# Moving the copies of two decode states from the ConvFFN stages into the prompt-attention stages

## The chip, the cores and the metric

The kernel runs on one core of one Trainium2 chip. The metric is device time in microseconds (us) for one execution, and a version is judged by its median over several runs.

## The reference

One inference step of a two-layer decoder trunk for a prompt (512 tokens) and a group of 8 samples with 8 new tokens each (T = 576 tokens in all). Layer 0 mixes with A (indexer-selected attention) and B (dilated windows), layer 1 with C (compressed, selected and sliding-window branches); each layer ends in a ConvFFN:

```
def conv_ffn(x, prev, w_up, conv_w, conv_b, w_down):
    n = x.shape[1]
    ext = jnp.concatenate([prev, x @ w_up], 1)
    ...
    return (jax.nn.gelu(gate) * val) @ w_down, ext[:, n:]
```

The step also returns its states, shifted by the 8 new rows. Only this part of the reference is what the change touches:

```
    kv_b = jnp.concatenate([state_kv, jnp.stack([kb, vb], 2)], 1)      # (8, 2048 + 8, 1024 floats)
    ... kv_b[:, -B_BUF:]                                               # s_b_kv, the last 2048 rows
    win = jnp.concatenate([state_win, kv[:, :, 4:]], 1)                # (8, 512 + 8, 256 floats)
    ... win[:, -C_BUF:]                                                # s_c_win, the last 512 rows
```

So 2040 rows of 4 KB for each of 8 samples of state_b (66.8 MB), and 504 rows of 1 KB for each sample of state_c (4.1 MB), are copied unchanged from one DRAM tensor to another. No engine computes with the copies.

## The kernel before

The kernel is a list of phases. Each opens its own SBUF and PSUM tiles and one block with a program for each engine (SyncE is SP, the others PE, DVE, ACT, POOL), and ends when every engine's program has ended: the semaphores are cleared, and all engines meet at a barrier (L97, L101). The order is: setup, projection of A and B, token-major rearrangement, indexers, sample attention B, sample attention A, prompt attention `pab`, output projection, `ffn0`, projection of C, rearrangement, compressed prompt branch, prompt attention `pc`, sample attention C, output projection, `ffn1`.

`ffn_phase` has an up part and a down part. The up part is a loop of LOOPS = 11 steps. A step has two slots s, and a slot holds 8 x 128 rows by 256 columns of w_up (1 MB, two loads of 512 KB by SP at L1633, tile `ffn_w`). ACT casts the slot to its high part (L1753, `ffn_wh`), DVE subtracts to get the low part (L208, `ffn_wl`), and PE forms three products for each (L216): 48 matmuls of 288 columns for each half slot, 192 in a step. SP may load a slot again as soon as DVE has split what was in it (`sp.wait_ge(w_low, ...)`). ACT may cast it as soon as PE has finished the slot's former content. ACT and DVE then do the convolution and the gate. The down part takes 22 pieces of w_down (512 KB each, SP at L1642, four slots), split in the same way (L1795, L208), and 30 matmuls of 512 columns for each (L1725 to L1727).

The copies are in the up part. At the start of each of the 11 steps ACT issues one DMA for four samples at once (L1558):

```
        e.dma_start(self.dst_b[self.b, bass.ds(i * self.ROWS, self.ROWS), :],
                    self.src_b[self.b, bass.ds(i * self.ROWS + NS, self.ROWS), :]).then_inc(self.copied, 16)
```

The access pattern is 4 samples x 185 rows x 4 KB. After the steps come a rest of 5 rows and the copy of state_c (L1564, L1565), and at the end of the phase ACT waits for them all. `ffn0` copies samples 0 to 3, `ffn1` samples 4 to 7.

`prompt_attention_phase` runs over 16 heads. In `pab` these are 8 heads of B and then 8 heads of A, with 4 query tiles each (per_head = 4). In `pc` each head has two branches (per_head = 8). PE computes logits (L560), DVE adds the bias from a table and takes the maximum (L639), ACT exponentiates (L620), PE turns (L571) and multiplies by the values (L588). SP loads a table of 1280 KB for each four heads and branch (L539), and for each head its queries, 128 KB in a ring of three slots (L543):

```
                if n >= 3:
                    sp.wait_ge(logit_ready, per_head * (n - 2))
                sp.dma_start(q[:, n % 3, :], hT[q_row:q_row + HD, 0:SEQ]).then_inc(q_in[n % 3], 16)
```

So the queries of head n are asked for when the logits of head n - 3 are done, two heads before PE needs them. After the last of them SP has nothing to do in the phase.

Of the kernel before, what the change touches and what calls it, by code (L numbers as in the profile page):

```python
# [26 lines left out]
NB, NS = 8, 8  # L27
# [5 lines left out]
PAST = 2048  # L33
PAGE = 128
LS = PAST + NS
HD = 64
# [36 lines left out]
class Phase:  # L73


    def __init__(self, nc, ctx, name):
        self.nc, self.ctx, self.name, self.sems = nc, ctx, name, []
        self.body = ExitStack()
# [405 lines left out]
                dve.tensor_tensor(s, s, keep.causal[:, :], ALU.add).then_inc(summed, 1)  # L484


def prompt_attention_phase(nc, name, branches, heads, hT, vec_up, tok, keep, tok_loads=(), sel_bias=None):

# [4 lines left out]
    with phase(nc, name) as p:  # L495
# [17 lines left out]
                 "weighed", "scaled", "mixed", "k_scaled")  # L513
        logit_ready, shifted_ready, probs_ready, turned, pT0, pT1, out_ready, weighed, scaled, mixed, k_scaled = (p.sem(n) for n in names)
        pT_ready = [pT0, pT1]
        k_in, v_in = p.sem("k_in"), p.sem("v_in")
        q_in = [p.sem(f"q_in{i}") for i in range(3)]
        t_in = [p.sem(f"table_in{i}") for i in range(2 * parts)]
        steps = [(n, i, part) for n in range(len(heads)) for i in range(NQ) for part in range(parts)]
# [3 lines left out]
        @block.sync  # L523
        def _(sp):
            for br, b in enumerate(branches):
                rows = hT[b["k"]:b["k"] + b["kv"] * HD, 0:SEQ].rearrange("(g e) t -> e g t", e=HD)
                sp.dma_start(kT[:, br, 0:b["kv"], :], rows).then_inc(k_in, 16)
            for n, (q_row, place, members) in enumerate(heads):
                if n == 1:
                    for dst, src in tok_loads:  # L530
                        sp.dma_start(dst, src).then_inc(v_in, 16)
                if n % 4 == 0:
                    g = n // 4
                    if g >= 2:
                        sp.wait_ge(shifted_ready, 4 * per_head * (g - 1))
                    for part, (br, h) in enumerate(members):
                        slot = (g % 2) * parts + part
                        head0 = (branches[br]["kind"] * N_HEADS + branches[br]["h0"] + h) * LU
                        sp.dma_start(table[:, slot, :, :], bass.AP(tensor=vec_up.tensor, offset=head0,  # L539
                                                                   ap=[[1, P], [LU, 4], [1, SEQ + P]])).then_inc(t_in[slot], 16)  # L540
                if n >= 3:
                    sp.wait_ge(logit_ready, per_head * (n - 2))
                sp.dma_start(q[:, n % 3, :], hT[q_row:q_row + HD, 0:SEQ]).then_inc(q_in[n % 3], 16)  # L543

        @block.tensor
        def _(pe):
# [999 lines left out]
class StateCopy:  # L1546

    ROWS = (PAST - NS) // (NF // 2)  # L1550

    def __init__(self, io, half, copied):
        self.src_b, self.dst_b, self.src_c, self.dst_c = io["state_b_kv"], io["o_s_b_kv"], io["state_c_kv"], io["o_s_c_win"]
        self.b, self.copied, self.before = slice(half * NB // 2, (half + 1) * NB // 2), copied, half * 16 * (NF // 2 + 2)

    def step(self, e, i):

        e.dma_start(self.dst_b[self.b, bass.ds(i * self.ROWS, self.ROWS), :],  # L1558
                    self.src_b[self.b, bass.ds(i * self.ROWS + NS, self.ROWS), :]).then_inc(self.copied, 16)

    def rest(self, e):

        done = self.ROWS * (NF // 2)
        e.dma_start(self.dst_b[self.b, done:PAST - NS, :], self.src_b[self.b, NS + done:PAST, :]).then_inc(self.copied, 16)  # L1564
        e.dma_start(self.dst_c[self.b, 0:C_WIN - NS, :], self.src_c[self.b, NS:C_WIN, :]).then_inc(self.copied, 16)  # L1565

    def wait(self, e):

        e.wait_ge(self.copied, self.before + 16 * (NF // 2 + 2))


def ffn_phase(nc, name, w_up, conv_w, conv_b, w_down, prev, g, b, p_tail, s_tail, y, state_copy, keep):

# [10 lines left out]
    with phase(nc, name) as p:  # L1586
# [172 lines left out]
        @block.scalar  # L1759
        def _(act):  # L1760
            act.wait_ge(up_done, 4)
            for s in range(2):
                split_high(act, s, 0, s)

            def step(i, ahead):

                state_copy.step(act, i)
                for s in range(2):
                    for e in (2 * s, 2 * s + 1):
                        act.wait_ge(up_done, i * 4 + (e + 5))  # L1770
                        act.wait_ge(conv3, i * 4 + (e + 1))
                        act.wait_ge(tails_out, i * 8 + 2 * (e + 1))
                        act.copy(ext[:, e, 2:2 + TH], acc[e][:, 0:TH]).then_inc(main_out, 1)
                    if ahead:
                        split_high(act, i * 2 + (s + 2), i + 1, s)
                    for e in (2 * s, 2 * s + 1):
                        act.wait_ge(main_out, i * 4 + (e + 5))
                        act.wait_ge(small_out, i * 8 + 2 * (e + 5))
                        act.wait_ge(prefix_in, i * 8 + 2 * (e + 1))
                        act.wait_ge(hid_done, i * 4 + 2 * (s + 1))  # L1780
                        act.activation(conv[:, e, :], ext[:, e, 0:CV], ACT.Identity, scale=par_slot[:, e, 0:1], bias=par_slot[:, e, 3:4]).then_inc(conv1, 1)
                    act.wait_ge(conv3, i * 4 + (2 * s + 5))
                    act.activation(gelu[:, s, :], conv[:, 2 * s, :], ACT.Gelu_apprx_tanh).then_inc(gelu_done, 1)

            with act.Fori(0, LOOPS - 1) as i:
                step(i, True)
            step(LOOPS - 1, False)
            state_copy.rest(act)
            act.wait_ge(hid_done, 4 + 2 * NF)
            for n in range(NF):  # L1790
                f2 = n % (NF // 2)
                down_slot_free(act, n)
                act.copy(hh[:, n % 3, :, 0:T], hid[:, 2 * f2:2 * f2 + 2, :]).then_inc(d_high, 1)  # L1793
                act.wait_ge(wd_in[n % 4], 16 * (n // 4 + 1))
                act.copy(wdh[:, n % 4, :, :], wd[:, n % 4, :, :]).then_inc(d_high, 1)  # L1795
                if 3 <= n < NF // 2 + 3:
                    m = n - 3
                    act.wait_ge(tail_turned, m + 1)
                    if m >= 2:
                        act.wait_ge(tail_stored[m % 2], 32 * (m // 2))  # L1800
                    act.copy(tail_rows[:, m % 2, :], acc2[1 + m % 2][0:NR, :]).then_inc(tail_out, 1)
                    act.wait_ge(tail_out, m + 1)
                    act.dma_start(p_tail[:, m * 512:(m + 1) * 512], tail_rows[0:2, m % 2, :]).then_inc(tail_stored[m % 2], 16)
                    act.dma_start(s_tail[:, m * 512:(m + 1) * 512], tail_rows[2:NR, m % 2, :]).then_inc(tail_stored[m % 2], 16)
            for t in range(NT):
                norm.root_of(act, t)
            for t in range(NT):
                norm.scale(act, t)
                if t >= 2 and y is None:
                    norm.high_part(act, t - 2, acc2[1:3])  # L1810
            if y is None:
                for t in range(NT - 2, NT):
                    norm.high_part(act, t, acc2[1:3])
            state_copy.wait(act)
            for m in range(2):
                act.wait_ge(tail_stored[m], 32 * len(range(m, NF // 2, 2)))

# [726 lines left out]
def build(nc, io):  # L2544
# [7 lines left out]
    with ExitStack() as ctx:  # L2552
# [7 lines left out]
        keep.causal = sb("causal", [P, P])  # L2560
        keep.chunk_row = sb("chunk_row", [P, NB], I32)
        keep.eps = sb("eps", [P, 1])
        copied = ctx.enter_context(nc.semaphore("state_copied"))
        const_in = ctx.enter_context(nc.semaphore("const_in"))

        keep.kidx_in = [ctx.enter_context(nc.semaphore(f"kidx_in{b}")) for b in range(NB)]
# [23 lines left out]
        with ExitStack() as ab:  # L2590
# [12 lines left out]
            with ExitStack() as pr:  # L2603
# [4 lines left out]
                    dict(heads=H_B, k=B_K, kv=H_B, v=P, kind=KIND_DIL, h0=8, sel=False, gate=None),  # L2608
                    dict(heads=H_A, k=A_K, kv=2, v=0, kind=KIND_FULL, h0=0, sel=True, gate=None),
                ], [(B_Q + h * HD, H_A + h, [(0, h)]) for h in range(H_B)] + [(A_Q + h * HD, h, [(1, h)]) for h in range(H_A)],  # L2610
                    dram.hT_ab, dram.vec_up, v_tok, keep, tok_loads=[
                    (v_tok[:, :, 0:P], io["o_p_a_kv"].rearrange("(i p) c -> p i c", p=P)[:, :, P:2 * P]),
                    (v_tok[:, :, P:], io["o_p_b_kv"][3 * SEQ:, :].rearrange("(i p) c -> p i c", p=P)[:, :, 512:D]),
                ], sel_bias=sel_bias)
        with x_parts(nc, keep, "x1"):
            output_phase(nc, "out_ab", io["w_out_ab"], io["ln1_g"][0], io["ln1_b"][0], keep)
            ffn_phase(nc, "ffn0", io["ffn_up"][0], io["ffn_conv_w"][0], io["ffn_conv_b"][0], io["ffn_down"][0], io["state_ffn"][0],
                      io["ln2_g"][0], io["ln2_b"][0], io["o_p_ffn"][0], io["o_s_ffn"][0], None, StateCopy(io, 0, copied), keep)

            project_phase(nc, "proj_c", io["w_in_c"], C_COLS, dram.hT_c, keep)  # L2620

        with ExitStack() as c:
# [6 lines left out]
            with nc.sbuf_tensor("mix_c", [P, NQ, D], F32) as mix:  # L2629
# [2 lines left out]
            prompt_attention_phase(nc, "pc", [  # L2632
                dict(heads=N_HEADS, k=C_KV + 2 * P, kv=2, v=3 * P, kind=KIND_FULL, h0=0, sel=False, gate=N_HEADS),
                dict(heads=N_HEADS, k=C_KV + 4 * P, kv=2, v=5 * P, kind=KIND_WIN, h0=0, sel=False, gate=2 * N_HEADS),
            ], [(C_Q + h * HD, h, [(0, h), (1, h)]) for h in range(N_HEADS)], dram.hT_c, dram.vec_up, tok, keep)
        sample_c_phase(nc, dram.hT_c, dram.vec, io["cache_c_kv"], io["state_c_kv"], io["o_s_c_kv"],
                       io["o_s_c_win"][:, C_WIN - NS:C_WIN, :], io, keep)
        with x_parts(nc, keep, "x2"):
            output_phase(nc, "out_c", io["w_out_c"], io["ln1_g"][1], io["ln1_b"][1], keep)
            ffn_phase(nc, "ffn1", io["ffn_up"][1], io["ffn_conv_w"][1], io["ffn_conv_b"][1], io["ffn_down"][1], io["state_ffn"][1],  # L2640
                      io["ln2_g"][1], io["ln2_b"][1], io["o_p_ffn"][1], io["o_s_ffn"][1], (io["o_y_prompt"], io["o_y_sample"]),
                      StateCopy(io, 1, copied), keep)


def t5_buckets(dist):
# [85 lines left out]
```

## Time and profile before

| | |
|---|---|
| time, 3 runs | 3455.67 us median, 3441.11 to 3469.64 |
| span of the profiled execution | 3459.9 us |
| PE busy | 2655.9 us (77%) |
| DVE / ACT / POOL busy | 1477.0 / 885.0 / 177.5 us |
| bytes moved by DMA | 344.26 MB, mean 100 GB/s |
| mean granted TensorE clock | 0.824 |

The profile gives no time of its own for the profiled execution beside its span. All times below are microseconds from the start of that span. The prompt attention `pab` runs from about 846 to 1032, `ffn0` from 1122 on, `pc` from about 1993 to 2304, and `ffn1` from 2822 to the end. The page cuts the span into 40 slices of 86.5 us and gives, in tenths, the busy share of an engine, the granted TensorE clock and the mean busy share of the 16 DMA engines.

### The profile page before, as it was taken

To read this page: it belongs to the slowest core of one execution; us is meant where nothing else is said; L and a number is where in the kernel's file an instruction comes from. 1 tells how busy PE (TensorE), PEld (TensorE's weight loads), DVE (VectorE), ACT (ScalarE), POOL (GpSimd) and SP (SyncE) were. 2 spreads that over 40 slices of the span, in tenths; PEclk is the share of its full clock that TensorE was granted. 3 is DMA by queue.
4 is the path that set the end of the run, shared out by engine and by line. 5 is a ranking of instruction groups with operands and counts; after the bars stand their busy time and mean duration, and the time that the engine had idled before them with its cause. 6 is when DMAs were issued, how large, how long until landed. Compare 5 with 4: busy or idle time off the path is not lost. (4 is left out here: it accounts for less than half of the span.)

```text
span 3459.9 us, 38384 instructions
## 1 busy us (share of the span) xinstructions
PE 2655.9 (77%) x13798; PEld 2027.6 (59%) x13802; DVE 1477.0 (43%) x2970; ACT 885.0 (26%) x1465; POOL 177.5 (5%) x404
## 2 busy tenths in 40 slices
PE   5976788686987777667967889977777777667596
PEld 2973333253556777666867745544555567667585
DVE  2223577555455333342342234654344433343334
ACT  1111111111232332233221122432323222333232
POOL 0000000000000111110000000000000011111000
PEclk9997788787588888879978556988889778888898
DMA  3352544222111433342123121133212123334321
GB/s 88 129 192 71 203 149 153 88 98 75 42 35 55 147 132 130 132 152 93 44 94 98 32 75 37 41 79 119 98 67 110 61 60 130 137 131 144 132 82 46
DMA packets 208838, 344.26 MB, mean 100 GB/s; under 512 B 32982, under 2 KB 144646, under 8 KB 204786
## 3 DMA queue, kind: packets, MB, share of 16 engines
q1 hardware_dynamic: 194992, 204.40, 19.5%
q10 hardware_dynamic: 10268, 83.75, 5.9%
q0 software_dynamic: 3456, 54.53, 4.1%
q8 instruction: 71, 1.16, 0.1%
q14 instruction: 51, 0.42, 0.0%
HBM read 315.74 MB, written 97.35 MB: 119 GB/s over the span
## 5 line engine op out<-in xcount | busy, mean ns | idle before, releaser
L216 PE MATMUL ffn_acc<-x_h,ffn_wh 128*128 128x288 f32 x1408 | 313.6, 306 | 217.5 <-DVE ffn_wl L208 217.5
L216 PEld LDWEIGHTS ffn_acc<-x_h,ffn_wh 128*128 128x128 f32 x1408 | 236.7, 197 | 220.0 <-issue 220.0
L208 DVE TENSOR_TENSOR ffn_wl<-ffn_w,ffn_wh 128x2048 fp32r<-128x2048 f32 (+1 forms) x88 | 154.4, 1754 | 410.8 <-ACT ffn_wh L1753 345.8
L216 PE MATMUL ffn_acc<-x_l,ffn_wh 128*128 128x288 f32 x1408 | 310.2, 303 | 0.0
L216 PE MATMUL ffn_acc<-x_h,ffn_wl 128*128 128x288 f32 x1408 | 309.5, 303 | 0.0
L216 PEld LDWEIGHTS ffn_acc<-x_l,ffn_wh 128*128 128x128 f32 x1408 | 236.0, 196 | 0.0
L216 PEld LDWEIGHTS ffn_acc<-x_h,ffn_wl 128*128 128x128 f32 x1408 | 235.2, 196 | 0.0
L1725 PE MATMUL ffn_acc<-ffn_wh,x_h 128*128 128x512 f32 x440 | 177.3, 403 | 69.2 <-DVE ffn_wl L208 69.2
L1726 PE MATMUL ffn_acc<-ffn_wl,x_h 128*128 128x512 f32 x440 | 174.6, 397 | 0.0
L1727 PE MATMUL ffn_acc<-ffn_wh,x_l 128*128 128x512 f32 x440 | 174.2, 396 | 0.0
L1753 ACT CAST ffn_wh<-ffn_w 128x2048 fp32r<-128x2048 f32 x44 | 84.0, 1910 | 316.8 <-DMA ffn_w<-ffn_up 316.8
L560 PE MATMUL pc_logit<-pc_kT,pc_q 64*128 64x128 f32 (+3 forms) x256 | 127.9, 589 | 15.7 <-DMA pc_q<-hT_c 15.7
L1725 PEld LDWEIGHTS ffn_acc<-ffn_wh,x_h 128*128 128x128 f32 x440 | 84.7, 193 | 87.6 <-DVE ffn_wl L208 40.5
L208 DVE TENSOR_TENSOR x_l<-ffn_hid,x_h 128x1152 fp32r<-128x1152 f32 x44 | 59.7, 1357 | 154.5 <-ACT x_h L1793 154.5
L639 DVE CUSTOM_DVE_ANT_0 pc_shifted<-pc_logit,pc_table 128x128 f32<-128x128 f32 (+3 forms) x128 | 62.7, 490 | 145.2 <-PE pc_logit L560 144.9
L620 ACT ACTIVATE pc_probs<-pc_shifted,pc_nmax 128x128 f32<-128x128 f32 (+3 forms) x128 | 71.9, 562 | 194.6 <-DVE pc_nmax L639 194.6
L588 PE MATMUL pc_out<-pc_pT,tok_c 128*64 128x128 f32 x640 | 118.9, 328 | 0.0
L2195 PE MATMUL sc_tps<-ident,sc_kv 128*128 128x128 f32 x384 | 67.5, 329 | 50.7 <-DMA sc_kv<-cache_c_kv,chunk_row 25.2
L1201 PE MATMUL sb_outp<-sb_v,sb_pT 128*64 128x512 f32 x160 | 91.4, 740 | 8.8 <-DVE sb_pT L1298 8.8
L588 PEld LDWEIGHTS pc_out<-pc_pT,tok_c 128*64 128x64 f32 x640 | 82.1, 162 | 25.7 <-issue 22.8
L1793 ACT CAST x_h<-ffn_hid 128x1152 fp32r<-128x1152 f32 x44 | 50.8, 1155 | 174.7 <-PE ffn_acc L1727 171.2
L1727 PEld LDWEIGHTS ffn_acc<-ffn_wh,x_l 128*128 128x128 f32 x440 | 84.6, 192 | 18.1
(404 smaller groups left out, 5123.5 us busy)
## 6 DMA issues: line engine op xcount, KB each, us to landing
out_s_b_kv<-state_b_kv ACTq DMA_DIRECT2D x22, 2960.0 KB
ffn_w<-ffn_up SPq DMA_DIRECT2D x88, 512.0 KB, 5.7
ffn_w<-ffn_down SPq DMA_DIRECT2D x44, 512.0 KB, 3.7
sb_k<-state_b_kv SPq DMA_DIRECT2D x8, 2048.0 KB, 13.2
sb_v<-state_b_kv SPq DMA_DIRECT2D x8, 2048.0 KB
proj_ab_w<-w_in_ab SPq DMA_DIRECT2D x11, 1024.0 KB, 5.4
pc_table<-vec_up SPq DMA_DIRECT2D x8, 1280.0 KB, 8.3
proj_c_w<-w_in_c SPq DMA_DIRECT2D x7, 1024.0 KB, 5.4
```

The lines of the kernel that those rows point to most:

```text
L208: return dve.tensor_tensor(low, whole, high.bitcast(F32), ALU.subtract)
L216: done = pe.matmul(o, weights, x, start=start, stop=stop)
L560: mm = pe.matmul(logit[s % 4][:, 0:L], q[:, n % 3, i * P:(i + 1) * P], kT[:, br, g, 0:L], start=True, stop=not sel)
L588: last = pe.matmul(out[n % 2][half * HD:(half + 1) * HD, i * P:(i + 1) * P], v, pT[:, s % 2, kt * P:(kt + 1) * P], start=(part == 0 and kt ...
L620: act.activation(probs[:, s % 4, 0:L], shifted[:, s % 4, 0:L], ACT.Exp, bias=nmax[:, s % 4:s % 4 + 1], scale=-1.0, accum_out=total[:, s % ...
L639: dve.tensor_tensor_reduce(out=shifted[:, s % 4, 0:L], in0=logit[s % 4][:, 0:L], in1=bias, scale=-1.0, scalar=FLOOR, op0=ALU.add, op1=ALU. ...
L1201: pe.matmul(outp[0:R, :], pT[:, t, :], v[:, b % 2, t, :], start=(t == 0), stop=False)
L1725: pe.matmul(down_acc[t][:, :], part[0], wide[0], start=(f == 0), stop=False)
L1726: pe.matmul(down_acc[t][:, :], part[0], wide[1], start=False, stop=False)
L1727: last = pe.matmul(down_acc[t][:, :], part[1], wide[0], start=False, stop=(f == NF - 1))
L1753: act.copy(wh[:, s, :, :], w[:, s, :, :]).then_inc(w_high, 1)
L2195: last = pe.transpose(tps[n % 2][0:rows, i * width:(i + 1) * width], src, keep.ident[:, :])
```

## The change

The copies are taken out of `ffn_phase` altogether. `prompt_attention_phase` takes a `StateCopy`, and SP issues one piece of the copy for each head: a quarter (510 rows) of one sample of state_b, as two DMAs of 510 rows x 2 KB, the left and the right half of the rows. With each fourth piece goes the copy of that sample's state_c (504 rows x 1 KB). Piece n - 2 is issued right after the queries of head n, so that piece 0 has no wait of its own before it. The last two pieces wait for the logits of heads 14 and 15, and at its end SP waits until all 36 copies of the phase have landed. `pab` copies samples 0 to 3, `pc` samples 4 to 7.

```diff
@@ prompt_attention_phase, block.sync
                 sp.dma_start(q[:, n % 3, :], hT[q_row:q_row + HD, 0:SEQ]).then_inc(q_in[n % 3], 16)
+                if n >= 2:
+                    state_copy.piece(sp, n - 2, copied)
+            for n in range(len(heads) - 2, len(heads)):
+                sp.wait_ge(logit_ready, per_head * (n + 1))
+                state_copy.piece(sp, n, copied)
+            sp.wait_ge(copied, 16 * state_copy.issued)
@@ class StateCopy
-    ROWS = (PAST - NS) // (NF // 2)
+    QUARTER = (PAST - NS) // 4
...
+    def piece(self, e, n, copied):
+
+        b, row = self.first + n // 4, n % 4 * self.QUARTER
+        for col in (0, 512):
+            e.dma_start(self.dst_b[b, row:row + self.QUARTER, col:col + 512],
+                        self.src_b[b, row + NS:row + NS + self.QUARTER, col:col + 512]).then_inc(copied, 16)
+        self.issued += 2
+        if n % 4 == 3:
+            e.dma_start(self.dst_c[b, 0:C_WIN - NS, :], self.src_c[b, NS:C_WIN, :]).then_inc(copied, 16)
+            self.issued += 1
@@ ffn_phase, block.scalar
-                state_copy.step(act, i)
...
-            state_copy.rest(act)
...
-            state_copy.wait(act)
```

## Rows read from the trace of the kernel before

**Rows 1.** Chain that ended last, up part of ffn1: start, us, what.

```profile
2837.01 33.79 DMA ffn_w<-ffn_up
2870.93 1.91 ACT ffn_wh L1753
...
2875.37 41.12 PE ffn_acc L216 x288
2916.72 31.48 another core or an unknown queue
```

**Rows 2.** Waits of PE, ffn0 and then ffn1: total us, times, longest.

```profile
PE ffn_acc L216 <- DVE ffn_wl L208: 108.2, 6, 23.8
PE ffn_acc L1725 <- DVE ffn_wl L208: 34.2, 2, 19.1
...
PE ffn_acc L216 <- DVE ffn_wl L208: 109.2, 6, 24.1
PE ffn_acc L1725 <- DVE ffn_wl L208: 34.9, 2, 20.8
```

**Rows 3.** Timeline of PE in ffn1: start, us, idle time before it in brackets.

```profile
2836.46 0.84 PE L216 MATMUL ffn_acc<-x_h,ffn_wh 128*128 128x288 f32 x2 [2.99 <-DVE ffn_wl L208]
...
3237.13 0.43 PE L216 MATMUL ffn_acc<-x_h,ffn_wl 128*128 128x288 f32 x2
3251.67 0.77 PE L1725 MATMUL ffn_acc<-ffn_wh,x_h 128*128 128x512 f32 x1 [14.12 <-DVE ffn_wl L208]
```

**Rows 4.** Windows: busy of PE, PEld, DVE, ACT, POOL; clock; DMA share; GB/s.

```profile
3012.00:3020.00 8.00, 0.00 (x0) 0.00 (x0) 0.00 (x0) 0.00 (x0) 0.00 (x0) 0.50 0.26 114
120.00:150.00 30.00, 30.00 (x227) 30.00 (x226) 6.87 (x7) 6.86 (x8) 0.00 (x0) 1.00 0.36 122
360.00:400.00 40.00, 18.30 (x65) 10.44 (x64) 19.18 (x29) 3.64 (x7) 0.00 (x0) 0.64 0.87 293
2970.00:3000.00 30.00, 30.00 (x227) 30.00 (x226) 14.17 (x22) 10.03 (x13) 3.49 (x16) 1.00 0.35 135
930.00:960.00 30.00, 30.00 (x83) 15.86 (x84) 12.30 (x43) 7.07 (x21) 0.00 (x0) 0.50 0.03 10
```

**Rows 5.** Timeline of PE in ffn0, after its first long wait.

```profile
1175.27 0.84 PE L216 MATMUL ffn_acc<-x_h,ffn_wh 128*128 128x288 f32 x2 [11.12 <-DVE ffn_wl L208]
...
1181.15 0.43 PE L216 MATMUL ffn_acc<-x_h,ffn_wh 128*128 128x288 f32 x2
```

**Rows 6.** Timeline of ACT and DVE between the two parts of ffn1.

```profile
3243.02 1.15 ACT L1793 CAST x_h<-ffn_hid 128x1152 fp32r<-128x1152 f32 x1 [1.78 <-DVE ffn_hid L1852]
3249.23 1.04 ACT L1795 CAST ffn_wh<-ffn_w 128x1024 fp32r<-128x1024 f32 x1 [5.05 <-DMA ffn_w<-ffn_down]
...
3250.30 1.23 DVE L208 TENSOR_TENSOR ffn_wl<-ffn_w,ffn_wh 128x1024 fp32r<-128x1024 f32 x1 [4.74 <-ACT ffn_wh L1795]
```

**Rows 7.** Timeline of SP's issues, pab and then pc: start, us from first to last.

```profile
931.91 38.42 SPq L543 DMA_DIRECT2D pab_q<-hT_ab  x4
978.00 24.88 SPq L543 DMA_DIRECT2D pab_q<-hT_ab  x4
...
2050.99 80.78 SPq L543 DMA_DIRECT2D pc_q<-hT_c  x4
2209.18 44.77 SPq L543 DMA_DIRECT2D pc_q<-hT_c  x4
```

**Rows 8.** Ends of pab and pc: last logits (tile view), then DVE's last.

```profile
L562 PE MATMUL pab_logit<-sel_bias,ident_bf x20: 282/336/392, 963.6 to 1026.4; 128*128 128x256 bf16 x8, 128*128 128x384 bf16 x8, 128*128 128x512 bf16 x4
1031.74 0.69 DVE L675 COPY mixT<-pab_out 64x512 f32<-64x512 f32 x1 [1.18 <-PE pab_out L588]
...
2303.17 0.69 DVE L673 TENSOR_TENSOR mixT<-pc_out,mixT 64x512 f32<-64x512 f32 x1 [1.20 <-PE pc_out L588]
```

**Rows 9.** DMA issues: count, KB each, median us from issue to landing.

```profile
pab_table<-vec_up SPq DMA_DIRECT2D x4, 1280.0 KB, 6.2
...
pab_q<-hT_ab SPq DMA_DIRECT2D x16, 128.0 KB, 2.5
```

More of the change, by code:

```diff
@@ L484, in _, with prompt_attention_phase @@
                 dve.tensor_tensor(s, s, keep.causal[:, :], ALU.add).then_inc(summed, 1)
-def prompt_attention_phase(nc, name, branches, heads, hT, vec_up, tok, keep, tok_loads=(), sel_bias=None):
+def prompt_attention_phase(nc, name, branches, heads, hT, vec_up, tok, state_copy, keep, tok_loads=(), sel_bias=None):
     with phase(nc, name) as p:
@@ L1546, with __init__, ffn_phase @@
 class StateCopy:
-    ROWS = (PAST - NS) // (NF // 2)
-    def __init__(self, io, half, copied):
+    QUARTER = (PAST - NS) // 4
+    def __init__(self, io, half):
         self.src_b, self.dst_b, self.src_c, self.dst_c = io["state_b_kv"], io["o_s_b_kv"], io["state_c_kv"], io["o_s_c_win"]
[L1554 to L1572, printed above, removed]
+        self.first, self.issued = half * NB // 2, 0
+    def piece(self, e, n, copied):
[7 more added lines that the diff above has]
+            self.issued += 1
+def ffn_phase(nc, name, w_up, conv_w, conv_b, w_down, prev, g, b, p_tail, s_tail, y, keep):
     EXT = 2 + SEQ + NB * (2 + NS)
@@ L2562, in build @@
         keep.eps = sb("eps", [P, 1])
-        copied = ctx.enter_context(nc.semaphore("state_copied"))
         const_in = ctx.enter_context(nc.semaphore("const_in"))
@@ L2610, in build @@
                 ], [(B_Q + h * HD, H_A + h, [(0, h)]) for h in range(H_B)] + [(A_Q + h * HD, h, [(1, h)]) for h in range(H_A)],
-                    dram.hT_ab, dram.vec_up, v_tok, keep, tok_loads=[
+                    dram.hT_ab, dram.vec_up, v_tok, StateCopy(io, 0), keep, tok_loads=[
                     (v_tok[:, :, 0:P], io["o_p_a_kv"].rearrange("(i p) c -> p i c", p=P)[:, :, P:2 * P]),
@@ L2617, in build @@
             ffn_phase(nc, "ffn0", io["ffn_up"][0], io["ffn_conv_w"][0], io["ffn_conv_b"][0], io["ffn_down"][0], io["state_ffn"][0],
-                      io["ln2_g"][0], io["ln2_b"][0], io["o_p_ffn"][0], io["o_s_ffn"][0], None, StateCopy(io, 0, copied), keep)
+                      io["ln2_g"][0], io["ln2_b"][0], io["o_p_ffn"][0], io["o_s_ffn"][0], None, keep)
             project_phase(nc, "proj_c", io["w_in_c"], C_COLS, dram.hT_c, keep)
@@ L2634, in build @@
                 dict(heads=N_HEADS, k=C_KV + 4 * P, kv=2, v=5 * P, kind=KIND_WIN, h0=0, sel=False, gate=2 * N_HEADS),
-            ], [(C_Q + h * HD, h, [(0, h), (1, h)]) for h in range(N_HEADS)], dram.hT_c, dram.vec_up, tok, keep)
+            ], [(C_Q + h * HD, h, [(0, h), (1, h)]) for h in range(N_HEADS)], dram.hT_c, dram.vec_up, tok, StateCopy(io, 1), keep)
         sample_c_phase(nc, dram.hT_c, dram.vec, io["cache_c_kv"], io["state_c_kv"], io["o_s_c_kv"],
@@ L2641, in build @@
                       io["ln2_g"][1], io["ln2_b"][1], io["o_p_ffn"][1], io["o_s_ffn"][1], (io["o_y_prompt"], io["o_y_sample"]),
-                      StateCopy(io, 1, copied), keep)
+                      keep)
 def t5_buckets(dist):
```

2 lines of the change are left out of this document (1 added, 1 removed).

## The prediction

> **What bounds the kernel now.** I read the chain of waits first. In the up part of ffn1 it goes round in one pattern: a load of `ffn_w` that takes 33.79 us to land, the cast on ACT, the split on DVE, 41 us of PE, and then 31.48 us that the view can't name [rows 1]. The same stretch in PE's timeline shows PE idle until DVE has split a slot, which waited for ACT, which waited for the load. The table of PE's waits sums this up: 108.2 us in six waits and 34.2 us in two in ffn0, 109.2 and 34.9 us in ffn1 [rows 2]. So PE sits idle for 286 us in the two ConvFFN stages, for want of weights.
>
> Whose fault is the late load? The windows tell. At 3012 to 3020 no engine is busy and the DMA share is 0.26 at 114 GB/s [rows 4]. A share of 0.25 is four engines of 16, all busy, and the copy is the one transfer whose outer dimension is 4 (its samples). It runs at about 114 / (16 x 0.26) = 27.4 GB/s an engine, and a copy of 3.03 MB needs about 28 us, which is the length of the unnamed wait. A weight load needs all 16 engines, the four with the copy among them, and is done when the last of them is. In the projection of A and B the same pattern of loads, casts and products runs with no copy beside it, and PE is busy for 30.00 of 30 us at a clock of 1.00 with 227 matmuls, at a DMA share of 0.36 [rows 4]. So the loads alone keep up.
>
> The Trainium skill's page "DMA: Bandwidth & Descriptors" (section on why a DMA increments its semaphore by 16) says that a DMA gets the largest number of engines up to 16 that divides the slowest dimension of both patterns. The share of 0.26 agrees for 4. For the new pieces of 510 rows it would give 15 engines, and the sum below would lose about 2 us by it.
>
> **What leaves ffn.** (a) Up part. The first wait of the six (2.99 us [rows 3]) is there at any rate, so 106.2 us of idle time can go in ffn1, and about 105.2 in ffn0. After each of the five other waits PE starts at half clock: from 1175.27 to 1181.15 it needs 5.88 us for 12 rows of two matmuls [rows 5], which at 30 / 227 = 0.132 us a matmul [rows 4] take 3.2. That is 2.7 us each, 13.5 in a stage. Gain 119.7 + 118.7. Check: ffn1's up part runs from 2836.46 to 3237.4 [rows 3], 400.9 us; 11 x 192 matmuls at 0.132 us are 279 and one slow start 3; the difference is 119.
>
> (b) Down part. Its first wait doesn't go away whole. With the load long there, `x_h` is cast from 3243.02 [rows 6], the weights' cast follows with 1.04 to 3245.2, DVE's split of `x_l` before and 1.23 of its own [rows 6] bring it to 3246.8, and PE begins near 3247.2, 9.7 us after the up part's end. So 14.12 [rows 3] shrinks by 4.4, and the second wait, 20.8 [rows 2], goes with its slow start of 2.4: 27.6 us in ffn1. In ffn0 34.2 - 9.7 + 2.4 = 26.9.
>
> (c) ACT issues 13 DMAs less in each stage and waits for none at the end. They lie beside PE's 6.3 us for a half slot, for which ACT waits anyway: nothing, and 13 x 0.7 = 9 us a stage if ACT were the bound.
>
> What is late next in ffn is PE itself, as in the projection. Sum of (a) and (b): 293 us.
>
> **What comes to the attention stages.** Each head brings SP two DMAs of 1.04 MB, with each fourth head one of 0.52 MB. The nearest row for lines of 2 KB is the load of state_b in sample attention: 293 GB/s at a share of 0.87 [rows 4], 337 GB/s with all engines. By that a head's 2.09 MB take 6.2 us. With the copy's own rate on 8 KB packets (27.4 GB/s an engine) it would be 4.8 us; I take 6.2, since the line length is the same. Queued before and behind it are the queries, 0.13 MB (0.4 us), and a share of a table, 6.2 / 4 = 1.55 us [rows 9]: 8.15 us a head of DMA time.
>
> A head lasts 38.42 / 3 = 12.8 us to 13.4 in the first half of pab and 24.88 / 3 = 8.2 in the second; in pc 26.8, later 14.8 [rows 7]. So the copies fit under the heads, with nothing to spare in pab's second half. The queries of head n + 1 queue behind piece n - 2 in SP's queue, but PE wants them two heads (16 us) later than they can be asked for, and 8 us of that is left. I put 2 us on it.
>
> What is bare is the end. The last piece may go only when the last logits are ready, about 1026.8 in pab [rows 8]. Then come 0.65 us of issue, (2.09 + 0.52) / 337 = 7.7 us of transfer, and about 2 us until the semaphore, as in the 2.5 us of a small load [rows 9]: 1037.2. DVE ends at 1032.4 [rows 8], so the barrier is 4.8 us later. In pc logits end at 2297.8, the copies at 2308.2, DVE at 2303.9 [rows 8]: 4.3 us. Cost 4.8 + 4.3 + 2 = 11 us.
>
> **The sum.** 293 - 11 = 282 us off the profiled 3459.9 gives 3178; that execution lies 4 us above the median of 3455.67, so the forecast is 3174 us. SP is not moved past anything but its own query and table loads, and POOL is not touched.
>
> **Rivals.**
>
> (A) The copies are slower with 16 engines than with four, since DRAM must then read and write at once. No row shows more than 293 GB/s counted once [rows 4]. If read and write together are held to that, a head's piece takes 2 x 2.09 / 293 = 14.3 us, with queries and table 16.3. Then the queries arrive late. pab becomes DMA-bound from the first piece at about 866: 16 x 16.3 and four state_c copies at 3.5 end near 1143 instead of 1032, 111 us. pc hides it in its slow heads, and pays 1.5 us on some 8 fast ones and 12 at the end: 25. Time 3456 - 293 + 136 = 3299. For it: the copy would need 674 GB/s of the memory, which nothing here has shown. Against it: the memory carries 228 (114 twice) from four busy engines without slowing them. Halfway, 10 us a head, costs some 15 us more than my forecast. The skill's page "DMA: Bandwidth & Descriptors" (Specifications) puts the limit of a core at about 358 GB/s, and counted for both directions that would be an estimated 11.7 us a head; no run here shows whether both count.
>
> (B) The other side, slower than before: the new pieces too get four engines or fewer, through the way in which 510 rows are dealt out. At 21 GB/s an engine [rows 4] four give 84 GB/s. A stage's 35.5 MB take 423 us, and these engines' share of queries and tables some 27 more: 450 against 186 for pab and 311 for pc. The excess, 264 + 139 = 403, eats the 293: 3456 + 110 = 3566. The point from which it decides is a stage of 395 us, about 96 GB/s, so fewer than five engines. Against it: the load of state_b has an outer dimension that isn't 4, and gets a share of 0.87.
>
> (C) The clock. In pab's first half TensorE has 0.50 (1.2 GHz) though it counts as busy for all of 30 us [rows 4], and pc's slow heads (those whose queries are asked for from 2050.99 to 2131.8 [rows 7]) have the same look; the stretch ends near 2135. Heads there take 13.4 and 26.8 us instead of 8.2 and 14.8. The change puts DMA work beside exactly these stretches, and a short wait of PE could end or lengthen them. If both vanished it would be 40 + 57 us less, 3077; if pc kept the low clock to its end, 11 heads x 12 = 132 more, 3306. For it: nothing that I see ends these stretches in pc. Against it: PE has no wait there that the copies would touch, and three runs differ by 28 us only.
>
> (D) The FFN doesn't speed up by as much since its own loads or ACT and DVE hold it: the projection's rows speak against that for the loads; between two long waits of ffn1, with the copies running, PE works 30.00 of 30 us while DVE works 14.17 and ACT 10.03 [rows 4], so these have room too. If they cost 3 us a step, 3174 + 66 = 3240.
>
> **How the numbers follow.** Forecast 0.68 (3150 to 3205, which takes in 4.8 to 8 us a head and tails of 2 to 10 us), A or part of it 0.12, B 0.05, C 0.09 (a third of it to the faster side), D 0.06. The range of 3125 to 3260 leaves out B, the full size of A and the outer thirds of C, some 0.2. Within 1% (about what a measurement can tell from no change) is the strip between B and the full A with a lengthened clock: 0.02. Slower by over 1%: 0.05. Faster: 0.93.
>
> **What the profile after would show.** PE's waits for `ffn_wl` in the up parts gone but the first, 192 matmuls in 25.4 us all through, the clock at 1.00, ffn0's and ffn1's up parts about 282 us each; about 10 us of idle time before the down part. In pab and pc: a DMA share near 0.8 in the fast heads, queries still landing before PE waits, and SP waiting for the copies for some 5 us after DVE's last instruction. I would be wrong if PE waits for `pab_q` again and again (A), if the share stands at 0.25 (B), or if the clock's low stretch has another length (C).

## The result and the profile after

The changed kernel takes 3182.06 us (median of 4 runs, 3161.59 to 3220.39), beside 3462.65 us for the kernel before. The ratio is 0.917, with a 95% interval of 0.910 to 0.925. The forecast was 3174, with a range of 3125 to 3260. In two later comparisons the same kernel had medians of 3196.0 and 3177.7 us. The ratios in this text compare undisturbed runs only, so that they don't follow from the medians alone.

The profiled execution has a span of 3159.8 us, 300.1 less than before. The head of its page:

```profile
span 3159.8 us, 38356 instructions
...
PE 2602.1 (82%) x13802; PEld 1989.1 (63%) x13802; DVE 1478.9 (47%) x2970; ACT 884.3 (28%) x1465; POOL 142.9 (5%) x404
...
PE   5996588868599769998959569994777776999896
...
PEclk9998588878755979999979668996888877999998
DMA  3444453232266422322212425736122112223221
```

Slices 16 to 18 and 35 to 37 of the 40 lie in the up parts of ffn: PE is busy for nine tenths or more, and its clock is at nine tenths or more. The DMA work has moved to slices 12 to 14 (pab) and 25 to 28 (pc). The table of PE's waits, in ffn0 and in ffn1, answers to [rows 2]:

```profile
PE ffn_acc L1726 <- DVE ffn_wl L208: 9.3, 1, 9.3
...
PE ffn_acc L216 <- DVE ffn_wl L208: 3.0, 1, 3.0
...
PE ffn_acc L1726 <- DVE ffn_wl L208: 9.3, 1, 9.3
PE ffn_acc L216 <- DVE ffn_wl L208: 3.0, 1, 3.0
```

Of 286.5 us idle time in 16 waits, 24.6 in four are left, and these are the ones that the prediction left there. The tile view gives the first loads of each stage (durations in ns, then start of the first and the last):

```profile
L1627 SPq DMA_DIRECT2D ffn_par_rows<-ffn_conv_w x2: 367/370/373, 1154.4 to 2666.1; - x2
L254 SPq DMA_DIRECT2D proj_c_w<-w_in_c x6: 372/375/388, 1641.5 to 1685.0; - x6
```

From such first loads every stage has a length. All are in us, each from one profiled execution:

| stage | before | after | difference |
|---|---|---|---|
| pab | 188.9 | 220.8 | +31.9 |
| ffn0 | 637.8 | 487.1 | -150.7 |
| pc | 312.7 | 271.3 | -41.4 |
| ffn1 | 637.2 | 493.7 | -143.5 |
| all others | 1683.3 | 1686.9 | +3.6 |

ffn gave 294.2 us. The attention stages, where only a cost was expected, moved by +31.9 and -41.4. Both have two parts. One is the bare end, here in pab, in the timelines of DVE and SP:

```profile
1057.03 0.69 DVE L681 COPY mixT<-pab_out 64x512 f32<-64x512 f32 x1 [1.18 <-PE pab_out L594]
...
1053.85 0.59 SPq L1569 DMA_DIRECT2D out_s_c_win<-state_c_kv  x1
1066.81 1.32 SPq L1470 DMA_DIRECT2D out_ab_w<-w_out_ab  x3
```

The last copy is issued at 1053.85. DVE is done at 1057.7, but the next stage's first load starts only at 1066.81, 9.1 us later, where it was 2.1 before [rows 8]. In SP's table of waits the reason stands by name:

```profile
SPq L97 <- DMA out_s_c_win<-state_c_kv: 10.1, 1, 10.1
```

In pc the same gap is 7.8 us instead of 1.9. The tails cost 7.0 and 5.8 us. The other part is the clock. The low-clock stretch lasts until about 1024 in pab instead of 966, and until about 1915 in pc, 40 us after its start instead of 140. A head takes 13.4 us at 1.2 GHz in pab and 14.8 us at 2.4 GHz in pc, just as before [rows 7], so the heads themselves are no slower for the copies beside them. With the tails taken off, the clock's part is +24.9 in pab and -47.2 in pc.

### The profile page after: what moved, and what is told of

Its sections match the earlier page's. It is cut to its first block and busy times, and to the rows that moved or that the text cites. A ratio compares the mean times of both kernels' runs of the same rounds, so it can differ in the third digit from the quotient of the medians.

```text
span 3159.8 us, 38356 instructions
## 1 busy us (share of the span) xinstructions
PE 2602.1 (82%) x13802; PEld 1989.1 (63%) x13802; DVE 1478.9 (47%) x2970; ACT 884.3 (28%) x1465; POOL 142.9 (5%) x404
## 5 line engine op out<-in xcount | busy, mean ns | idle before, releaser
L216 PE MATMUL ffn_acc<-x_h,ffn_wh 128*128 128x288 f32 x1408 | 300.8, 295 | 6.0 <-DVE ffn_wl L208 6.0
L216 PE MATMUL ffn_acc<-x_l,ffn_wh 128*128 128x288 f32 x1408 | 300.3, 295 | 0.0
L216 PE MATMUL ffn_acc<-x_h,ffn_wl 128*128 128x288 f32 x1408 | 300.2, 295 | 0.0
L216 PEld LDWEIGHTS ffn_acc<-x_h,ffn_wh 128*128 128x128 f32 x1408 | 226.9, 189 | 6.2 <-issue 6.2
L216 PEld LDWEIGHTS ffn_acc<-x_l,ffn_wh 128*128 128x128 f32 x1408 | 226.9, 189 | 0.0
L566 PE MATMUL pc_logit<-pc_kT,pc_q 64*128 64x128 f32 (+3 forms) x256 | 108.0, 506 | 16.0 <-DMA pc_q<-hT_c 16.0
L1834 DVE COPY ffn_ext<-ffn_acc 128x224 f32<-128x224 f32 x88 | 34.2, 388 | 169.5 <-PE ffn_acc L216 169.5
L594 PE MATMUL pc_out<-pc_pT,tok_c 128*64 128x128 f32 x640 | 100.7, 290 | 0.0
L566 PE MATMUL pab_logit<-pab_kT,pab_q 64*128 64x128 f32 (+3 forms) x128 | 82.0, 741 | 20.5 <-DMA pab_q<-hT_ab 20.5
L2193 PEld LDWEIGHTS sc_tps<-ident,sc_kv 128*128 128x128 f32 x384 | 53.8, 172 | 68.6 <-DMA sc_kv<-cache_c_kv,chunk_row 30.3
```

The lines of the kernel that those rows point to most:

```text
L216: done = pe.matmul(o, weights, x, start=start, stop=stop)
L566: mm = pe.matmul(logit[s % 4][:, 0:L], q[:, n % 3, i * P:(i + 1) * P], kT[:, br, g, 0:L], start=True, stop=not sel)
L594: last = pe.matmul(out[n % 2][half * HD:(half + 1) * HD, i * P:(i + 1) * P], v, pT[:, s % 2, kt * P:(kt + 1) * P], start=(part == 0 and kt ...
L2193: last = pe.transpose(tps[n % 2][0:rows, i * width:(i + 1) * width], src, keep.ident[:, :])
```

## The experiments

All kernels of one comparison ran on one chip, each beside the kernel before. Stage lengths are read as above.

**The changed kernel again (e0_after_again).** No edit.

> The changed kernel as it is, beside the others on the same chip, to have its time and a second trace of the low-clock stretches. Expected: 3182 us within 1%. If the length of the low-clock stretches varies from run to run (theory), pab's and pc's differ from the first trace (about 160 us and 30 us) by tens of us while ffn0, ffn1 and the two tails agree within 2 us; if they are set by the program (rival), they agree within some us.

Measured: 3196.0 us (3181.6 to 3212.2), ratio 0.921 (0.914 to 0.928). The profiled execution has pab 226.1 and pc 306.6 us (220.8 and 271.3 in the first trace), ffn0 494.3 and ffn1 493.9. So pc differs by 35 us between two executions of one kernel, and its low-clock stretch lasted until about 2005, 120 us. The two gaps at the ends agree within 0.3 us with the first trace. The expected agreement of ffn0 within 2 us failed (494.3 against 487.1); the last section comes back to it.

**No copies at all (e1_no_copies).**

```diff
-                if n >= 2:
-                    state_copy.piece(sp, n - 2, copied)
-            for n in range(len(heads) - 2, len(heads)):
-                sp.wait_ge(logit_ready, per_head * (n + 1))
-                state_copy.piece(sp, n, copied)
-            sp.wait_ge(copied, 16 * state_copy.issued)
```

> This kernel leaves out all copies of state_b and state_c (the 2040 and 504 unchanged rows of each sample are not written). It gives what the copies cost in the attention stages. Theory 1 (they cost only the bare tail at the end of each stage, 7.0 us in pab and 5.8 us in pc by the trace after): about 13 us less than the changed kernel, near 3165 us, with pab and pc as long as after but for the tails, if the low-clock stretches are as long; ffn0 and ffn1 487 and 494 us as after. Rival (the copies also slow the heads, through late queries or through the memory): the heads themselves get shorter than 13.4 us at the low clock and 8.2 us at the high one in pab, and the gain is 30 us or more. If the length of the low-clock stretches is set by the copies, pab's goes back to the 100 us of before.

Measured: 3189.8 us (3166.7 to 3196.5), ratio 0.920 (0.912 to 0.927), which can't be told from the changed kernel's 3196.0. The gaps at the ends of pab and pc are 2.2 and 2.0 us, so the tails are the copies'. ffn0 and ffn1 take 494.5 and 491.0. The low-clock stretch in pab lasted until about 1025 though nothing is copied there: such a long stretch does not need the copies. As it happens, it is as long as in the changed kernel's first trace (181 us), and so is pc's as in e0_after_again (120 us), so that the stages can be compared at equal clock: pab takes 213.9 us, which is 220.8 less the tail of 7.0, and pc takes 300.8, which is 306.6 less 5.8. 71 MB of copies, read and written, cost the changed kernel the two tails and nothing else that shows. The times as a whole (6 us apart, where 13 were expected) are too coarse to show that.

**Copies back in ffn, one DMA for each sample (e2_ffn_spread).** From the kernel before:

```diff
-    ROWS = (PAST - NS) // (NF // 2)
+    ROWS = 176
...
-        e.dma_start(self.dst_b[self.b, bass.ds(i * self.ROWS, self.ROWS), :],
-                    self.src_b[self.b, bass.ds(i * self.ROWS + NS, self.ROWS), :]).then_inc(self.copied, 16)
+        for b in self.samples:
+            e.dma_start(self.dst_b[b, bass.ds(i * self.ROWS, self.ROWS), :],
+                        self.src_b[b, bass.ds(i * self.ROWS + NS, self.ROWS), :]).then_inc(self.copied, 16)
```

> The copies stay where they were, in the up parts of ffn, issued by ACT at the start of each step, but one DMA for each sample (176 rows of 4 KB) instead of one for four samples (4 x 185 rows). Theory 1 (the loss was the spread: four engines full of copy, and each weight load needs all 16): the up parts run without waits of PE, about 282 us instead of 401, the DMA share goes to 0.6 in them, and the time is about that of the changed kernel, 3150 to 3190 us. Rival (the place: copy bytes beside weight loads delay these, however they are spread): PE still waits for most of 100 us in each ffn, and the time stays at 3400 us or above.

Measured: 3196.4 us (3185.5 to 3198.0), ratio 0.922 (0.915 to 0.928). That is the changed kernel's time, with the copies where they always were. Windows of the up part of ffn0, with the same columns as [rows 4]:

```profile
1210.00:1240.00 30.00, 30.00 (x227) 30.00 (x226) 18.63 (x26) 14.14 (x18) 3.60 (x17) 1.00 0.52 169
1240.00:1270.00 30.00, 30.00 (x227) 30.00 (x226) 17.02 (x28) 13.54 (x16) 4.92 (x20) 1.00 0.67 222
1270.00:1300.00 30.00, 30.00 (x227) 30.00 (x226) 15.19 (x25) 15.37 (x19) 4.14 (x20) 1.00 0.66 232
```

PE is never idle while DMA moves up to 232 GB/s, more than before the change. So copy bytes beside weight loads were not what made the loads late. Only the wait before the down part is longer, 12.5 and 12.7 us instead of 9.3.

**The same with only the order of the axes changed (e8_ffn_rows185, e9_ffn_rows176).** One DMA a step by ACT as before, with the rows outermost. The second has 176 rows for 185, and its two last copies are turned too:

```diff
-        e.dma_start(self.dst_b[self.b, bass.ds(i * self.ROWS, self.ROWS), :],
-                    self.src_b[self.b, bass.ds(i * self.ROWS + NS, self.ROWS), :]).then_inc(self.copied, 16)
+        e.dma_start(self.dst_b[self.b, bass.ds(i * self.ROWS, self.ROWS), :].rearrange("b r c -> r b c"),
+                    self.src_b[self.b, bass.ds(i * self.ROWS + NS, self.ROWS), :].rearrange("b r c -> r b c")).then_inc(self.copied, 16)
```

> The copies as in the kernel before, in ffn, one DMA a step by ACT, the same 4 samples x 185 rows x 4 KB, with one thing changed: the rows are the outer dimension and the samples the inner one. Theory 1 (the dealing out over engines follows the outer dimension, as the skill's page DMA: Bandwidth & Descriptors says for the largest divisor up to 16, so 185 = 5 x 37 gives five engines): five engines at 27 GB/s carry a copy in 22 us instead of 28; two copies and the loads' share keep them busy for some 58 of the 51 us that PE needs for two steps, so PE still waits, but for 20 to 50 us in each ffn instead of 106, and the copies alone show a DMA share of 0.31. Rival (the rows are dealt out over all engines whatever their number): no waits in the up parts, as in the kernel with 176 rows.

Measured in one execution: 3247.1 us, ffn0 542.0 and ffn1 542.2. PE's waits over the whole kernel:

```profile
PE ffn_acc L216 <- DVE ffn_wl L208: 78.5, 16, 8.5
PE ffn_acc L1725 <- DVE ffn_wl L208: 21.8, 2, 11.0
```

Without the first waits of 3.0, 72.5 us are left for both up parts, 36 each. It was 106 with the samples outermost, so one permutation of the axes took away 96 us of each ffn. The expected 20 to 50 us was met. No window of this trace has the copy alone, so its share can't be read, but the engines can be counted. The traces have one packet of 4 bytes for each engine that carries a part of a DMA, and the page counts them under 512 B. (In e2_ffn_spread 16 packets of a copy are under way at once, and its 104 copies leave 1664 = 104 x 16 such small ones.) The line of the page for the kernel without copies (e1_no_copies), the kernel before, this one and the changed kernel:

```profile
DMA packets 207254, 273.28 MB, mean 86 GB/s; under 512 B 32878, under 2 KB 144542, under 8 KB 204682
...
DMA packets 208838, 344.26 MB, mean 100 GB/s; under 512 B 32982, under 2 KB 144646, under 8 KB 204786
...
DMA packets 223732, 344.26 MB, mean 106 GB/s; under 512 B 33004, under 2 KB 144668, under 8 KB 221088
...
DMA packets 241110, 344.26 MB, mean 109 GB/s; under 512 B 33966, under 2 KB 145630, under 8 KB 238410
```

The kernel before has 32982 - 32878 = 104 more than the one without copies: 26 copies on four engines. This kernel has 22 more than that: its 22 turned copies run on five engines. The changed kernel has 1088 more than the one without copies: 64 pieces of state_b on 15 engines and 8 of state_c on 16.

> As the kernel with the rows outermost and one DMA a step by ACT, with 176 rows instead of 185 (176 = 16 x 11; what is left goes with the rest at the end). Theory 1 (sixteen engines): no waits of PE in the up parts but the first of 3 us, each ffn 494 to 498 us as with one DMA for each sample, time about 3185 us. Rival (it was the number of DMAs, four small ones instead of one big one, that let the loads through in the kernel with one DMA a sample): PE waits as before the change, time near 3450.

Measured: 3142.3 us (3119.7 to 3176.2), ratio 0.924 (0.915 to 0.933). ffn0 494.3, ffn1 491.0. Waits of PE in ffn0, and a window of its up part:

```profile
PE ffn_acc L1726 <- DVE ffn_wl L208: 9.3, 1, 9.3
...
PE ffn_acc L216 <- DVE ffn_wl L208: 3.0, 1, 3.0
...
1180.00:1210.00 30.00, 30.00 (x228) 30.00 (x227) 15.89 (x27) 13.85 (x16) 4.63 (x20) 1.00 0.69 216
```

The waits are those of the changed kernel. As the DMAs are as many and nearly as large as before the change, it is not their number either. Nor is it the size of the packets, which the turned axes change too: the kernels with 185 and 176 rows both move state_b in packets of 4,096 bytes, on five and on 16 engines, with 36 and 0 us of waits, and the kernel before and e2_ffn_spread in packets of 47,360 and 45,056 bytes, on four and on 16, with 106 and 0 us. What counts is over how many engines one DMA is dealt out.

**Four engines in the attention stages (e3_attn_four).** From the changed kernel:

```diff
-        for col in (0, 512):
-            e.dma_start(self.dst_b[b, row:row + self.QUARTER, col:col + 512],
-                        self.src_b[b, row + NS:row + NS + self.QUARTER, col:col + 512]).then_inc(copied, 16)
+        s, row = slice(self.first, self.first + NB // 2), n * P
+        rows = min(P, PAST - NS - row)
+        e.dma_start(self.dst_b[s, row:row + rows, :], self.src_b[s, row + NS:row + NS + rows, :]).then_inc(copied, 16)
```

> The copies are in the attention stages, one piece a head as after the change, but each piece is one DMA of 4 samples x 128 rows x 4 KB (2.1 MB, and one such DMA of state_c at the end). This is the rival of the prediction in which the pieces get four engines. Theory 1 (four engines at the 27 GB/s each that the copies had in ffn): 33.4 MB need 306 us in each stage, with state_c and the share of the loads some 345 us, against 221 and 271 us after: about 3370 us, so still faster than before, with a DMA share near 0.25 in both stages. Theory 2 (21 GB/s an engine, as the prediction took for this rival): 450 us a stage, about 3560 us, slower than before. Rival (the number of engines does not matter in this place, since the heads leave room): within 30 us of the changed kernel.

Measured: 3419.1 us (3413.9 to 3533.8), ratio 0.987 (0.978 to 0.996). pab takes 365.7 and pc 377.2 us. Windows of pab:

```profile
1060.00:1160.00 100.00, 53.08 (x187) 30.91 (x189) 24.66 (x81) 13.45 (x41) 0.00 (x0) 0.59 0.26 109
1160.00:1205.00 45.00, 0.00 (x0) 0.00 (x0) 0.00 (x0) 0.00 (x0) 0.00 (x0) 0.50 0.22 94
```

The share is back at a quarter, PE is half idle, and for the last 45 us the stage only waits for copies. PE's waits for queries rise from one of 20.5 us to 12 of 107.1:

```profile
PE pab_logit L566 <- DMA pab_q<-hT_ab: 107.1, 12, 20.2
PE pc_logit L566 <- DMA pc_q<-hT_c: 32.5, 5, 16.2
```

Almost all of the gain is given back: the move alone, with the old access pattern, is worth 1.3%. The price of 450 us a stage was too high, that of 345 somewhat low.

**All pieces at once (e6_attn_burst).** All 16 pieces of a stage follow the queries of head 2.

> All 16 pieces of a stage are issued at once behind the queries of head 2, so that the queries of head 3 queue behind 35.5 MB of copies. It measures the copy's top rate on many engines. Theory 1 (the engines are the limit, 21 to 23 GB/s each on 15 engines): the burst takes 103 to 113 us in each stage, at over 310 GB/s, and PE waits some 80 us in pab for the queries of head 3. Rival (rival A of the prediction: memory holds read and write together to 293 GB/s): it takes 240 us, at about 147 GB/s.

Measured in one execution: 3296.4 us. Windows of pab; in the last PE is idle, waiting for the queries of head 3:

```profile
858.00:868.00 10.00, 10.00 (x26) 4.72 (x24) 4.94 (x21) 4.07 (x13) 0.00 (x0) 0.50 1.01 332
...
880.00:890.00 10.00, 10.00 (x29) 5.18 (x27) 3.46 (x13) 1.74 (x6) 0.00 (x0) 0.50 0.99 332
920.00:940.00 20.00, 0.00 (x0) 0.00 (x0) 0.00 (x0) 0.00 (x0) 0.00 (x0) 0.50 0.98 333
```

```profile
853.03 20.96 SPq L1563 DMA_DIRECT2D out_s_b_kv<-state_b_kv  x8
...
957.35 3.36 SPq L1567 DMA_DIRECT2D out_s_c_win<-state_c_kv  x1
960.76 0.59 SPq L543 DMA_DIRECT2D pab_q<-hT_ab  x1
```

The second fence is SP's timeline: the first copy is issued at 853.03, and the queries of head 3 at 960.76. PE waits 82.9 us for the latter, as expected. The copies run at 332 GB/s for 100 us, 664 GB/s if reading and writing are both counted. On 15 engines that is 22 GB/s each. That settles rival A. The share is no count of engines here: it reads up to 1.01 although each of these copies leaves 15 small packets, since the times of the packets of 2 KB overlap (up to 19 are under way at once). The Trainium skill's page "DMA: Bandwidth & Descriptors" (Specifications) has some 358 GB/s a core for the memory, which is half of the 716 GB/s of a stack. Here the sum of reading and writing went far above the 358, and stayed below the 716; so in this run, where one core was at work, the figure for a core did not bound both together.

**Rows of 4 KB (e5_attn_4kb).** One DMA of 510 x 4 KB a piece for two of 510 x 2 KB.

> The piece of a head is one DMA of 510 rows x 4 KB instead of two of 510 rows x 2 KB. Theory 1 (how long a row is hardly matters, since the heads hide the transfer): stages and tails as after, within 2 us at equal clock, the DMA share in the attention stages a little lower. Rival (2 KB rows matter): with 4 KB rows, queries or tables land later and PE waits, or the tail changes by more than 3 us. A time for its own between 3160 and 3220 us either way.

Measured in one execution: 3204.7 us, pab 223.6, pc 304.4, gaps at the ends 6.5 and 5.6 us instead of 9.1 and 7.8. Window of pab, first the kernel with 4 KB and then the changed one:

```profile
900.00:930.00 30.00, 30.00 (x86) 16.55 (x85) 11.72 (x40) 6.69 (x22) 0.00 (x0) 0.50 0.51 178
```

```profile
900.00:930.00 30.00, 30.00 (x86) 16.53 (x85) 12.02 (x42) 7.25 (x23) 0.00 (x0) 0.50 0.65 196
```

178 / 0.51 against 196 / 0.65 is 349 against 302 GB/s for a share of 1. The whole rows move some 16% more for the same packet time and shorten each tail by 2.6 and 2.2 us, a little more than the 2 us expected. The heads don't change. The experiment changes more than the length of a row, though. 510 whole rows lie one behind the other in DRAM, and the trace shows such a piece as 32 packets of 65,280 bytes, with 16 small packets for 16 engines, where two pieces of half rows are 1,020 packets of 2,048 bytes on 15 engines. Which of the two makes the difference was not taken apart. The half rows of the change bring nothing; they cost a little.

**Pieces earlier (e4_attn_early, e10_early_five, beside e11_after_five).**

```diff
-                if n >= 2:
-                    state_copy.piece(sp, n - 2, copied)
-            for n in range(len(heads) - 2, len(heads)):
-                sp.wait_ge(logit_ready, per_head * (n + 1))
-                state_copy.piece(sp, n, copied)
+                for m in {0: (), 1: (), 2: (0, 1), 3: (2, 3)}.get(n, (n,)):
+                    state_copy.piece(sp, m, copied)
```

> The pieces of the changed kernel come earlier: two each with the queries of heads 2 and 3, one with each later head, so that the last is issued three heads before the end. Theory 1 (the copies cost only the bare tails, 7.0 and 5.8 us over what a stage's end takes without them): DVE's last instruction of pab and pc is followed by the next stage's first load after 2 us, as before the change, instead of 9.1 and 7.8, the heads are as long as after (13.4 us at the low clock, 14.8 us in pc at the high one), and the kernel is 13 us faster than the changed one, near 3180 us beside its 3196 in the last comparison. Rival (two pieces at once delay the queries): PE waits for queries in the first heads and gives the gain back.

Measured: 3161.8 us (3153.8 to 3169.5), ratio 0.922 (0.913 to 0.932). DVE ends pab at 1055.0, and the next load starts at 1057.20: 2.2 us. The double pieces hold SP's issues up for up to 11 us early in the stage, but PE has no new wait for queries. The tails are gone. To see it in time, this kernel and the changed one were run again, six times each:

> The kernel with the earlier pieces again, beside the changed kernel on the same chip and in more rounds. Theory 1 (its stages are shorter by the two bare tails, 13 us): 13 us (0.4%) below the changed kernel's time, 9 to 17 us. Rival (the low-clock stretches vary by more than that between runs): the two medians differ by anything between -20 and 40 us, and only the stages of the traces tell the 13 us.

> The changed kernel beside the kernel with the earlier pieces, in as many rounds. Expected 3182 us within 1%, each ffn 494 us, DVE's last instruction of pab followed by the next stage's first load after 9 us.

Measured: 3182.5 us (3144.7 to 3197.8), ratio 0.934 (0.923 to 0.944), for the earlier pieces and 3177.7 us (3128.8 to 3213.5), ratio 0.926 (0.917 to 0.935), for the changed kernel. Inconclusive in time: the spread of one kernel is 85 us, and the 13 us that the stages show drown in it. e9_ffn_rows176, which has no tails either, had the lowest median of that comparison, but its runs overlap those of the changed kernel, so no version is shown to be faster than the change.

**The kernel before again (e7_before_again).**

> The kernel before, as it is, for a second trace. Theory 1 (the low-clock stretches of pab and pc vary from run to run, and no change to the copies sets them): their lengths differ from the first trace (about 100 us in pab, 128 us in pc) by tens of us, while each ffn stage is again 638 us. Rival (without copies in it, pab's stretch is short): again about 100 us in pab.

Measured in one execution: 3434.1 us; pab 188.9 again, pc 288.8 instead of 312.7, ffn0 639.7, ffn1 636.6. For pab alone the rival holds. But e9_ffn_rows176, e2_ffn_spread and e8_ffn_rows185 have the same code in pab, with no copies in it, and took 166.3, 209.4 and 219.3 us there. SP's timelines in pab, first e9 and then e2, give the time for the queries of four heads at about the same place:

```profile
928.69 23.87 SPq L543 DMA_DIRECT2D pab_q<-hT_ab  x4
960.23 24.88 SPq L543 DMA_DIRECT2D pab_q<-hT_ab  x4
```

```profile
929.62 41.54 SPq L543 DMA_DIRECT2D pab_q<-hT_ab  x4
984.80 36.11 SPq L543 DMA_DIRECT2D pab_q<-hT_ab  x4
```

Over three heads that is 8.0 and 8.3 us a head at 2.4 GHz, against 13.8 at 1.2 GHz and 12.0 where the clock rises on the way. So the stretch takes any length from 72 to 195 us in pab without copies in it. In the changed kernel and the ones with earlier or contiguous pieces, six traces, it takes 171 to 195. The copies are not needed for a long stretch; whether they keep it from being short, these few traces can't tell. What sets it stays open.

## Why the prediction was right, and where it was not

**Late weights.** Right. PE's idle time for weights was the whole gain: 293 us were forecast, 294.2 measured in ffn. That the two agree within 1 us is luck in part: ffn0 took 487.1 us in that trace, and 494.1 to 494.6 in seven of the nine traces without copies in ffn. With 494.3 there the gain is 287 us, 6 less than forecast.

**Whose fault.** The prediction read four engines out of a share of 0.26 and held them, not the bytes, to be the cause. The kernels with turned axes show it: 106, 36 and 0 us of waits in an up part for outer dimensions of 4, 185 and 176, counted as 4, 5 and 16 engines, at the same place and nearly the same bytes. What the prediction did not draw from this is that the move is not needed: the new access pattern is what pays.

**(a) and (b).** The waits and the slow starts go as worked out, but the up part itself was put slightly too short: 282 us were reckoned, and 283 to 284 is what it takes in most traces (in the first, 276.2 in ffn0 and 284.4 in ffn1). That is some 4 of the 6 us. Before the down part 9.7 us were to remain and 9.3 did, and the second wait went.

**Cost in attention.** 11 us were forecast: 9.1 for the tails and 2 for late queries. The tails are 12.8 and the queries nothing. The size of the tail was off, not its mechanism: the last state_c copy is issued at 1053.85, in 0.59 us, and SP waits 10.1 us more for it, so it lands at about 1064.5, 12.4 us after the last logits at 1052.1, where 10.4 were reckoned. The sum had one issue of 0.65 us in it, and there are three of 0.83, 0.83 and 0.59. The rate was right: 337 GB/s were taken from another load, and the burst ran at 332. The other value that the prediction weighed, 27.4 GB/s an engine, it put down to packets of 8 KB; in the trace they are of 47,360 bytes.

One sign did not come: the DMA share was to be near 0.8 in the fast heads. It is 0.61 in pc's (2000 to 2090), whose 14.8 us leave more room than the 8.2 that the 0.8 belongs to, and 0.50 in pab (1026 to 1052), where the clock rose only for the last three heads.

**Rival A** is refuted by the burst, at 332 GB/s counted once. **Rival B** fell twice. The new pieces don't get four engines but 15, as the small packets tell, the number that the prediction gave beside its sum. And when they are given four, the kernel is 1.3% faster than before, not 3% slower, since four engines carry 109 GB/s in large packets (the 94 of the second window include the end of the copies), where the prediction took 84 from rows of 2 KB. The mechanism is as described, with queries late by 107 us in pab, but its price was mis-sized. **Rival D**: 227 matmuls in 30 us with copies and weights together leave nothing for it.

**Rival C, the clock,** came about in both directions in one execution, +24.9 in pab and -47.2 in pc. pc's is within what one and the same kernel does from trace to trace. For pab it is not shown that the change has no part in it. The stretches vary between executions, so they belong in the range of any kernel of this program. The prediction's argument against them, that three runs differ by 28 us only, was too weak: runs of the kernel before went from 3382 to 3501 us in the last comparison.

## What to carry to other kernels

Before moving a transfer that makes others late, read the DMA share while it runs alone. Here a share of 0.26 meant four engines of 16, and loads that need all 16 waited for these four. With small packets the share says less (it read 0.99 for 15 engines), and the count of packets under 512 B, beside that of a kernel without the transfer, is the surer sign. A permutation of its axes that puts a dimension divisible by 16 outermost may do what a move does. The background copies that were spread over 15 or 16 engines cost the PE-bound stages nothing here, but the last piece should be issued a few heads before the end of a stage that waits for it. Where the spread of runs is larger than the effect, compare stages between traces: the ffn stages, whose clock is steady, agreed within 3 us in the nine traces without copies in ffn, but for ffn0 in two of them.

## What the runs showed of the hardware

- A DRAM-to-DRAM copy on four engines, in packets of 47,360 to 65,536 bytes, runs at 109 to 114 GB/s, some 27 an engine. Copies with 510 rows of 2 KB outermost run at 332 GB/s, counted once, on 15 engines, 22 an engine.
- Outer dimensions of 4, 185, 510 and 176 gave 4, 5, 15 and 16 engines, counted by the packets of 4 bytes.
- The length of the stretch at 1.2 GHz at the start of a prompt-attention stage varies from about 70 to 195 us in pab and from 40 to 150 in pc (the burst and the four-engine kernel, which make PE wait there, aside), between executions and with the same code, at a PE that counts as fully busy. At 5 us for each head of 13.4 in pab and 12 for each of 26.8 in pc, this alone moves the kernel by an estimated 90 us (120 / 13.4 x 5 + 110 / 26.8 x 12). Long and short stretches came without copies in the stage. What ends it was not found.
- In the up part of ffn0, at a granted clock of 1.00, PE ran 233 matmuls in 30 us in two traces of the changed kernel and 227 in a third (e0_after_again). First e11_after_five, then e0_after_again:

```profile
1290.00:1320.00 30.00, 30.00 (x233) 30.00 (x232) 15.56 (x27) 13.44 (x16) 4.16 (x21) 1.00 0.29 79
```

```profile
1290.00:1320.00 30.00, 30.00 (x227) 30.00 (x227) 15.39 (x27) 12.41 (x15) 4.21 (x19) 1.00 0.30 82
```

  That is 2.6% for the up part, and the 7 us by which ffn0 differs (487.1 and 487.4 against 494.3). The cause stays open.
